# Neighbourhood attention: probabilities turned unscaled, outputs multiplied once a pair by spread inverse sums, turned copies on two engines

## The reference, cut to what matters

```
q = split(rmsnorm(z[..., :D].reshape(B, L, H, dh), q_g) * (dh ** -0.5))
k = split(rmsnorm(z[..., D:2 * D].reshape(B, L, H, dh), k_g))
v = split(z[..., 2 * D:])
cstart = np.clip(col - kw // 2, 0, GRID_W - kw)
...
s = einsum('bhqd,bhrqwd->bhqrw', q_i, k_win) + bias
pr = softmax(s over the 8 x 16 keys of a query)
o = einsum('bhqrw,bhrqwd->bhqd', pr, v_win)
```

## Time and profile before

| what | value |
|---|---|
| time, median of 3 runs | 3695.46 us (3694.06 to 3698.54) |
| span of the profiled execution | 3695.6 us, 56005 instructions |
| PE busy | 3392.3 us, 92% |
| DVE busy | 1827.5 us, 49% |
| ACT busy | 1101.2 us, 30% |
| mean granted TensorE clock | 0.957 of full |
| neighbourhood attention: first score to last keep | about 3153 to 3224.5 us of the span |

### The profile page before, as it was taken

The page is one execution under the profiler, slowest core; times in us unless marked ns, Lnnn a source line. Parts: engine busy times, 40 slices in busy tenths (PEclk is TensorE's granted clock), DMA queues, the critical chain, the costliest instruction groups (busy, mean ns, idle before and its releaser), DMA issues. The chain is left out here.

```text
span 3695.6 us, 56005 instructions
## 1 busy us (share of the span) xinstructions
PE 3392.3 (92%) x23970; PEld 2377.8 (64%) x23970; DVE 1827.5 (49%) x2876; ACT 1101.2 (30%) x1833; POOL 249.3 (7%) x204
## 2 busy tenths in 40 slices
PE   7889789999888988999989788879999999899999
PEld 6577543332667753333267787747888879588887
DVE  3655433222466443332254666466664552866645
ACT  3543300000345330000032433114333432643333
POOL 1011000000101100000020222101000100010001
PEclk9899999999989998999999899979999998999999
DMA  5031279999402126999942000012222221122222
GB/s 215 12 115 69 94 298 428 427 427 428 189 32 109 75 85 286 428 427 427 428 182 81 3 3 3 3 43 97 92 92 89 96 112 46 52 110 96 92 80 80
DMA packets 49815, 595.87 MB, mean 161 GB/s; under 512 B 5376, under 2 KB 7680, under 8 KB 14080
## 3 DMA queue, kind: packets, MB, share of 16 engines
q1 hardware_dynamic: 49568, 592.29, 39.7%
HBM read 590.17 MB, written 2.10 MB: 160 GB/s over the span
## 5 line engine op out<-in xcount | busy, mean ns | idle before, releaser
L601 PE MATMUL psum<-source_hi,weights_hi 128*128 128x512 f32 (+1 forms) x2352 | 918.2, 390 | 63.2 <-DVE weights_lo L502 55.2
L601 PE MATMUL psum<-source_lo,weights_hi 128*128 128x512 f32 (+1 forms) x2352 | 909.4, 387 | 0.0
L601 PE MATMUL psum<-source_hi,weights_lo 128*128 128x512 f32 (+1 forms) x2352 | 908.7, 386 | 0.0
L601 PEld LDWEIGHTS psum<-source_hi,weights_hi 128*128 128x128 f32 x2352 | 447.6, 190 | 160.1 <-DVE weights_lo L502 66.2
L601 PEld LDWEIGHTS psum<-source_lo,weights_hi 128*128 128x128 f32 x2352 | 448.0, 190 | 89.5 <-issue 2.6
L601 PEld LDWEIGHTS psum<-source_hi,weights_lo 128*128 128x128 f32 x2352 | 447.5, 190 | 89.0
L502 DVE TENSOR_TENSOR weights_lo<-weight_ring,weights_hi 128x1024 fp32r<-128x1024 f32 (+4 forms) x286 | 337.9, 1187 | 303.5 <-ACT weights_hi L455 302.8
L455 ACT CAST weights_hi<-weight_ring 128x1024 fp32r<-128x1024 f32 (+4 forms) x286 | 286.4, 1009 | 668.1 <-PE psum L601 658.0
L1606 DVE TENSOR_TENSOR x<-psum,x 128x512 f32<-128x512 f32 x256 | 164.1, 684 | 202.8 <-PE psum L1486 202.8
L1453 PE MATMUL psum<-weight_ring,branches 128*64 128x512 f32 x1024 | 232.9, 597 | 8.9 <-DMA weight_ring<-in_w_up 4.8
L1453 PE MATMUL psum<-weight_ring_first,branches 128*64 128x512 f32 x1024 | 232.9, 597 | 7.1 <-DMA weight_ring_first<-in_w_up 4.0
(11 more groups left out here) (371 smaller groups left out, 4464.7 us busy)
## 6 DMA issues: line engine op xcount, KB each, us to landing
lent_weights<-in_w_down SPq DMA_DIRECT2D x64, 2048.0 KB, 17.2
weight_ring_first<-in_w_gate SPq DMA_DIRECT2D x32, 2048.0 KB, 16.6
weight_ring<-in_w_up SPq DMA_DIRECT2D x32, 2048.0 KB, 17.7
weight_ring<-in_w_gate SPq DMA_DIRECT2D x32, 2048.0 KB, 16.9
weight_ring_first<-in_w_up SPq DMA_DIRECT2D x32, 2048.0 KB, 18.3
weight_ring<-in_ffn_w_up SPq DMA_DIRECT2D x22, 2048.0 KB, 7.8
weight_ring<-in_ffn_w_down SPq DMA_DIRECT2D x8, 2048.0 KB, 7.8
weight_ring<-in_mix_w_in SPq DMA_DIRECT2D x6, 2048.0 KB, 8.2
```

The costliest lines, as they stand in the source:

```text
L601: ins = pe.matmul(ps, a, b, start=k == 0 and q == 0, stop=k == job.rows // P - 1 and q == 2)
```

## The change

The exponentials are no longer scaled: turn(j) waits for them directly. The reciprocals of the sums of all tiles of a pair go to a tile `inv`. When the outputs of a pair are whole, ACT copies them from bank 6 (now the only output bank) to `sums` (`copy_out`). PE spreads the inverse sums: `share(p)` multiplies the broadcast column of `inv` with the identity for each of the 4 query tiles and 2 heads, which leaves in bank 7, for every feature row and query column, the inverse sum of that query. `keep(p)` multiplies the two. The copies of turned blocks are shared: even j stay on ACT, odd j are made by DVE, at step j + 1, behind row_max(j + 3); the last one comes after the loop.

```diff
--- before.py
+++ after.py
@@ -2759,13 +2759,18 @@
     with ExitStack() as ctx:
         prob = K.sbuf(ctx, "probs", [P, 4, 2, W])
         probT = K.sbuf(ctx, "probs_t", [P, 2, TT, 2, 2, P])
-        st = K.sbuf(ctx, "softmax_stats", [P, 4, 8])
+        st = K.sbuf(ctx, "softmax_stats", [P, 4, 6])
+        inv = K.sbuf(ctx, "inverse_sums", [P, 2 * TT, 2])
+        sums = K.sbuf(ctx, "unscaled_output", [P, 2, T])
         table = K.sbuf(ctx, "bias_tables", [P, 2, 2, 2, W])
-        (block, (scores, dlink, biased, nmax_ready, exp_done, prob_ready, turned, turned_kept, out_ready, out_kept,
+        (block, (scores, biased, nmax_ready, exp_done, inverse, turned, kept_act, kept_dve, out_ready, out_copied, out_kept, spread,
                  landed0, landed1)) = ctx.enter_context(stage(
-                     nc, "scores_ready", "dve_link", "scores_biased", "neg_max_ready", "exp_done", "probs_ready",
-                     "probs_turned", "turned_kept", "output_ready", "output_kept", "bias_landed0", "bias_landed1"))
-        MAX, NMAX, SUM, INV = (slice(2 * i, 2 * i + 2) for i in range(4))
+                     nc, "scores_ready", "scores_biased", "neg_max_ready", "exp_done", "inverse_sums_ready",
+                     "probs_turned", "turned_kept_act", "turned_kept_dve", "output_ready", "output_copied", "output_kept", "inverse_sums_spread", "bias_landed0",
+                     "bias_landed1"))
+        kept = kept_act, kept_dve
+        MAX, NMAX, SUM = (slice(2 * i, 2 * i + 2) for i in range(3))
+        OUT, SHARE = 6, 7
 
         @block.sync
         def _(sp):
@@ -2791,9 +2796,9 @@
 
             def turn(j):
                 if j >= 2:
-                    pe.wait_ge(turned_kept, j - 1)
+                    pe.wait_ge(kept[j % 2], j // 2)
                 for a in range(2):
-                    pe.wait_ge(prob_ready, 2 * j + a + 1)
+                    pe.wait_ge(exp_done, 2 * j + a + 1)
                     for s in range(2):
                         at = (2 * a + s) * P
                         ins = pe.transpose(K.psum[:, 4 + j % 2, at:at + P], prob[:, j % 4, a, s * P:(s + 1) * P], K.ident)
@@ -2801,16 +2806,27 @@
 
             def out(j):
                 p, qt = divmod(j, TT)
-                pe.wait_ge(turned_kept, j + 1)
-                if p >= 2 and qt == 0:
-                    pe.wait_ge(out_kept, p - 1)
+                if p and qt == 0:
+                    pe.wait_ge(out_copied, p)
+                pe.wait_ge(kept[j % 2], j // 2 + 1)
                 for s, tile in enumerate(key_tiles(qt)):
                     for a in range(2):
-                        ins = pe.matmul(K.psum[rows(a), 6 + p % 2, qt * P:(qt + 1) * P],
+                        ins = pe.matmul(K.psum[rows(a), OUT, qt * P:(qt + 1) * P],
                                         v[:, tile, (2 * p + a) * HEAD:(2 * p + a + 1) * HEAD],
                                         probT[:, p % 2, qt, a, s, :], start=s == 0, stop=s == 1)
                 if qt == TT - 1:
                     ins.then_inc(out_ready, 1)
+
+            def share(p):
+                pe.wait_ge(inverse, TT * (p + 1))
+                if p:
+                    pe.wait_ge(out_kept, p)
+                for qt in range(TT):
+                    for a in range(2):
+                        ins = pe.matmul(K.psum[rows(a), SHARE, qt * P:(qt + 1) * P],
+                                        inv[:, (TT * p + qt) % (2 * TT), a:a + 1].to_broadcast([P, HALF]), K.ident,
+                                        start=True, stop=True)
+                ins.then_inc(spread, 1)
 
             score(0)
             score(1)
@@ -2820,12 +2836,13 @@
                 turn(j)
                 if j:
                     out(j - 1)
+                if j % TT == 1 and j // TT >= 1:
+                    share(j // TT - 1)
             out(n - 1)
+            share(pairs - 1)
 
         @block.vector
         def _(dve):
-            link = linker(dve, dlink)
-
             def row_max(j):
                 b = j % 4
                 p, qt = divmod(j, TT)
@@ -2833,6 +2850,7 @@
                 dve.wait_ge((landed0, landed1)[p % 2], 16 * (p // 2 + 1))
                 if j >= 4:
                     dve.wait_ge(turned, j - 3)
+                    dve.wait_ge(inverse, j - 3)
                 for a in range(2):
                     dve.tensor_tensor_reduce(out=prob[:, b, a, :], in0=K.psum[:, 2 * (j % 2) + a, 0:W],
                                              in1=table[:, p % 2, qt // (TT - 1), a, :], scale=1.0, scalar=-3.0e38,
@@ -2841,25 +2859,37 @@
                 dve.tensor_scalar(st[:, b, NMAX], st[:, b, MAX], -1.0, None, ALU.mult).then_inc(nmax_ready, 1)
 
             def keep(p):
-                dve.wait_ge(out_ready, p + 1)
-                src = K.psum[:, 6 + p % 2, :].rearrange("p (c r) -> p c r", c=GRID_W)
+                dve.wait_ge(out_copied, p + 1)
+                dve.wait_ge(spread, p + 1)
+                src = sums[:, p % 2, :].rearrange("p (c r) -> p c r", c=GRID_W)
+                by = K.psum[:, SHARE, :].rearrange("p (c r) -> p c r", c=GRID_W)
                 to = by_rows(q[:, p, :])
-                dve.tensor_copy(to[:, 8:, :], src[:, 0:GRID_W - 8, :])
-                dve.tensor_copy(to[:, 0:8, :], src[:, GRID_W - 8:, :]).then_inc(out_kept, 1)
+                dve.tensor_tensor(to[:, 8:, :], src[:, 0:GRID_W - 8, :], by[:, 0:GRID_W - 8, :], ALU.mult)
+                dve.tensor_tensor(to[:, 0:8, :], src[:, GRID_W - 8:, :], by[:, GRID_W - 8:, :], ALU.mult).then_inc(out_kept, 1)
+
+            def copy(j):
+                p, qt = divmod(j, TT)
+                dve.wait_ge(turned, j + 1)
+                if p >= 2 and qt == 1:
+                    dve.wait_ge(out_ready, p - 1)
+                dve.tensor_copy(probT[:, p % 2, qt].rearrange("p a s q -> p (a s q)"), K.psum[:, 4 + j % 2, :])\
+                    .then_inc(kept_dve, 1)
 
             row_max(0)
             row_max(1)
             for j in range(n):
                 b = j % 4
                 dve.wait_ge(exp_done, 2 * (j + 1))
-                link(dve.reciprocal(st[:, b, INV], st[:, b, SUM]))
-                for a in range(2):
-                    dve.tensor_scalar(prob[:, b, a, :], prob[:, b, a, :], st[:, b, 6 + a:7 + a], None, ALU.mult)\
-                        .then_inc(prob_ready, 1)
+                if j >= 2 * TT:
+                    dve.wait_ge(spread, j // TT - 1)
+                dve.reciprocal(inv[:, j % (2 * TT), :], st[:, b, SUM]).then_inc(inverse, 1)
                 if j + 2 < n:
                     row_max(j + 2)
+                if j % 2 == 0 and j:
+                    copy(j - 1)
                 if j % TT == 2 and j // TT >= 1:
                     keep(j // TT - 1)
+            copy(n - 1)
             keep(pairs - 1)
 
         @block.scalar
@@ -2877,13 +2907,23 @@
                 if p >= 2 and qt == 0:
                     act.wait_ge(out_ready, p - 1)
                 act.copy(probT[:, p % 2, qt].rearrange("p a s q -> p (a s q)"), K.psum[:, 4 + j % 2, :])\
-                    .then_inc(turned_kept, 1)
+                    .then_inc(kept_act, 1)
+
+            def copy_out(p):
+                act.wait_ge(out_ready, p + 1)
+                if p >= 2:
+                    act.wait_ge(out_kept, p - 1)
+                act.copy(sums[:, p % 2, :], K.psum[:, OUT, :]).then_inc(out_copied, 1)
 
             exponential(0)
             for j in range(n):
                 if j + 1 < n:
                     exponential(j + 1)
-                copy(j)
+                if j % 2 == 0:
+                    copy(j)
+                if j % TT == 0 and j:
+                    copy_out(j // TT - 1)
+            copy_out(pairs - 1)
 
 
 def neighbourhood(K, q, k, v):
```

## The result

| | before | after |
|---|---|---|
| median of 4 runs, us | 3694.93 (3694.06 to 3698.54) | 3712.37 (3711.47 to 3715.2) |
| ratio, 95% interval | 1 | 1.0048 (1.0035 to 1.0061) |
| span of the profiled execution, us | 3695.6 | 3710.7 |
| the stage, us | 71.8 | 89.4 |

The change makes the kernel slower by 17.4 us; +18.6 us and 3714 were forecast. A fourth run of before has moved its median from 3695.46 to 3694.93. The stage is measured from ACT's table load ahead of its first exponentials (3153.04 before, 3151.09 after) to the first cast of the next stage (3224.83, 3240.51): +17.6 us, the whole of the difference of the medians. The two profiled spans differ by 15.1 only, since the stretches outside the stage, which nobody changed, came out 2.5 us shorter in this execution.

The account below looks back on a forecast made before the run. PE was taken to set the plain step at 1.81 us; 15.9 + 7.3 - 4.6 - 0.5 - 0.7 + 1.2 = +18.6 us gave 3714.1, predicted as 3714. The mechanism's range was widened to 3707 to 3722; the stated range was 3705 to 3727.

Parts of the forecast that it names:

- stalls of out behind the copy: Even steps j = 2 to 28: PE's out(j-1) waits behind score, row maximum and DVE's copy; 1.17 us each, 15.9 total.
- share in the loop: PE's added matmuls, 1.04 us per pair with nothing hiding them; seven in the loop, +7.3 us.
- keep stalls and the tail's waits gone: Turn no longer waits for DVE's scaling: six stalls of 0.77 us go, 4.6, and 0.5 for the seventh in the tail.
- start: Start of the stage: the first turn no longer waits for a reciprocal and a scaling; -0.7 us once.
- end: End of the stage: share and its latency between last out and keep, slower last copy and keep; +1.2 us (1.0 to 1.6).
- keep's product, copy_out and the extra waits are hidden: DVE and ACT beside PE's stalls: keep's product, ACT's copy_out and the reciprocal's link waits cost nothing in the loop.
- The first stall: First of the fourteen stalls of out, where the clock is still half; 0.7 us instead of 1.17.
- the per-stall and share bounds: Stalls at 14 x 0.95 to 14 x 1.3 us and share at 0.88 to 1.2 a pair; total from 3709 to 3718.
- that of no stall: Rival: the copy gets through before PE reaches out(j-1), PE stays the bound; 3697.7 us, chance 8%.
- that of PE following DVE: Rival: PE's 1.81 us step is only DVE's rhythm, share fits PE's slack; 3686.7 us, chance 3%.
- The falling clock: Rival: regular gaps of about 1 us on PE drop the clock to half in the stage; 3754 or 3734, chance 9%.
- a busy stretch at full clock: Evidence against the clock's fall: at 886 to 896 us PE is busy 8.0 of 10 at the full 2.4 GHz.

Follow-up runs that it names:

- e1: The changed kernel with DVE's copy(j-1) put ahead of row_max(j+2) instead of behind it; 3695.01 us, ratio 1.0001.
- e3: The kernel before with only the odd turned copies moved to DVE, behind row_max(j+2), scaling kept and no share; 3709.66 us, ratio 1.0044.
- e7: The changed kernel with DVE's turned copy made twice, first into a spare tile; 3736.45 us, ratio 1.0113.
- e8: e1 with share moved from behind out(j-1) to between score and turn of the next step; 3695.71 us (1 run).
- e5: e1 with share's eight matmuls made twice over the same bank; 3703.83 us, ratio 1.0026.

## Why the prediction was right, step by step

| step | forecast us | measured us | where it shows |
|---|---|---|---|
| stalls of out behind the copy | 13 x 1.17 + 0.7 = 15.9 | 14 x 1.16 = 16.2 | transposes to out 1.75 (3188.15 to 3189.90) against 0.59 |
| share in the loop | 7 x 1.04 = 7.3 | 7 x 0.87 = 6.1 | 3190.49 to 3193.17 less 1.81 |
| keep stalls and the tail's waits gone | -4.6 - 0.5 | -(6 x 0.76 + 0.51 + 0.47) = -5.5 | no wait of turn for DVE; tail below |
| start | -0.7 | -0.8 | first row maximum to first turn 1.99 against 2.75 |
| in no term | 0 | +0.30 + 0.20 = +0.5 | table load to first row maximum 4.27 against 3.97; score to turn(2) 0.89 (3161.64 to 3162.53) against 0.69 |
| end | +1.2 | +1.05 | below |
| sum | +18.6 | +17.6 | stage +17.6 |

The rows for the start and end in the kernel after:

```profile
3155.36 0.42 DVE L2855 CUSTOM_DVE_ANT_0 probs<-psum,bias_tables 128x256 f32<-128x256 f32 x1 [4.61 <-DMA bias_tables<-in_na_bias]
...
3157.35 1.11 PE L2804 MATMUL psum<-constants,probs 128*128 128x128 f32 x4
```

and at its end:

```profile
3237.49 0.66 PE L2814 MATMUL psum<-probs_t,second_block_tiles 128*64 128x128 f32 x8 [0.20 <-DVE probs_t L2875]
...
3239.14 0.91 DVE L2867 TENSOR_TENSOR second_block_tiles<-unscaled_output,psum 128x448 f32<-128x448 f32 x1 [1.70 <-PE psum L2826]
```

Before, the last out ran 0.70 us ahead of keep, now 1.65; the last copy on DVE adds 0.1. The last two turns of the kernel before, which in the kernel after wait for nothing:

```profile
3219.80 0.63 PE L2799 MATMUL psum<-constants,probs 128*128 128x128 f32 x4 [0.46 <-DVE probs L2857]
...
3221.45 0.63 PE L2799 MATMUL psum<-constants,probs 128*128 128x128 f32 x4 [0.43 <-DVE probs L2857]
```

Turn to turn took 1.69 and 1.65 there; now it is 1.18 each, share not counted.

The mechanism was right in place, count and size: e1 removes it with two lines moved, e3 makes it alone, and e7's second copy lengthens each even step by its own 0.61. That keep's product, copy_out and the extra waits are hidden was right too: in e1, which has them all, PE is never late for them, and DVE's product takes 0.93 us for 448 columns where 0.97 was taken. The same copy out of PSUM took 585 ns on ACT and 687 on DVE in the kernel after, which decided nothing. It agrees in sign with the Trainium skill ("VectorE: DVE Perf Modes", table at its head), which places ScalarE closer to PSUM.

Three sizes were off. Share was taken 0.17 too dear a pair, because a fixed cost was given to each group that belongs, by e8, to a change of tile shape; that is 1.2 us of the 18.6. The first stall was taken at 0.7 for the half clock; the clock had risen by then and it is 1.16 (turn 3162.53, out 3164.28). And the tail held two waits of turn for DVE, not one: in j = 30 no score is left ahead of the turn, so turn(30) comes earlier and waits for its scaling too; 0.98 went instead of 0.5. The +0.5 that no term had, a later bias table and a score still partly at the half clock, hides this last one in the sum, so that part of the agreement is luck.

The working has slips that moved nothing. Keep's parts add to 3.6 and not 3.3, though 3.29 is what it came to (3193.17 to 3196.46), 0.43 ahead of the next row maximum. DVE loses 0.61 us of scaling a step, not 1.2, which is two steps. Fourteen copies at ACT's duration would save 1.3 us and not 1.4, and the per-stall and share bounds reach down to 3710, not 3709. Of the two ranges given, 3707 to 3722 and 3705 to 3727, no sum leads to the second; 3712.37 lies in both.

Of the rivals, that of no stall falls by the waits, that of PE following DVE by e5 and e1, where PE has no slack for share. The falling clock had 9%; it did not come in the kernel after (clock 1.00 in its window, and half only at the start of the stage, as before the change), and came in e7 with the longer wait of PE (0.84). The row that was held against it, a busy stretch at full clock, spoke rightly for the kernel after. The Trainium skill ("TensorE: Matmul & The Clock Gate", section "A second HAM failure mode: psum-queue depth-cycling") describes such a swing from short idles between groups; e7 agrees with it and the kernel after doesn't show it.

## What to carry to other kernels

When a piece of work moves to another in-order engine, write down what stands ahead of it there and whose output that waits for: if it is the output of the engine that waits for the moved piece, a circle is closed in every step, and no idle time on either engine helps. Here DVE lost 19.7 us of scalings in the stage and gained 11.0 us of copies, 1.1 us less work a pair, and the kernel got slower; the cure was the order of two lines. A normalisation put off to the end isn't free where the engine that then spreads the factors sets the pace: here it cost 0.87 us a pair.

## What the runs showed of the hardware

- A group of matmuls with another tile shape than the one before starts about 0.15 us late on this kernel's PE; one with the same shape follows at once: share 0.87 us behind out, 1.02 between score and turn (one run), and three changes fewer in two steps give 0.50.
- TensorE's clock fell from regular short gaps: it was 1.00 with a gap of 1.1 us in every second step, 0.84 with 1.7, and 1.00 again once 0.9 us of useless transposes filled the longer gap, and the kernel was 12.5 us faster for them.
